# Expert weights through three pairs of buffers to the end, token rows in a ring of four, gate and up halves as 16 KB rows

## The reference, cut to what matters

```
for e in range(N_EXPERTS):                    # 32 experts, 520 tokens, D_MODEL 1024, D_EXPERT 256
    gu = xt @ w_gate_up[e]                    # 1024 x 512, f32: 2 MiB
    h = silu(gu[:, :D_EXPERT]) * gu[:, D_EXPERT:]
    y = y + gate[:, e:e + 1] * (h @ w_down[e])    # 256 x 1024, f32: 1 MiB
return layernorm(ALPHA * x1 + y)
```

## Time and profile before

| | us |
|---|---|
| median of 3 runs | 604.76 |
| the three runs | 601.89, 604.76, 605.17 |
| the profiled execution, its time | 602.56 |
| its span, first to last instruction | 600.9 |

### The profile page before, as it was taken

The page is one execution under the profiler, slowest core; times in us unless marked ns, Lnnn a source line. Parts: engine busy times, 40 slices in busy tenths (PEclk is TensorE's granted clock), DMA queues, the critical chain, the costliest instruction groups (busy, mean ns, idle before and its releaser), DMA issues.

```text
span 600.9 us, 8960 instructions
## 1 busy us (share of the span) xinstructions
PE 518.8 (86%) x3296; PEld 281.0 (47%) x3296; DVE 373.2 (62%) x722; ACT 191.4 (32%) x356; POOL 134.0 (22%) x156
## 2 busy tenths in 40 slices
PE   5999999999979879899999898888887777767761
PEld 4887788874355443445556743333332222222220
DVE  1642059898933576652258666677886477666686
ACT  0100374214243644121142122444444244432340
POOL 1001054500025760000000201233323222221231
PEclk9999999999979999999999899999999899999997
DMA  9940008570606932001978599999999999999951
GB/s 302 405 155 6 1 1 331 213 269 1 279 5 230 395 116 87 2 1 59 417 290 342 180 420 406 409 396 419 415 415 411 419 418 419 415 415 418 401 193 43
DMA packets 34010, 157.95 MB, mean 263 GB/s; under 512 B 12680, under 2 KB 12680, under 8 KB 20016
## 3 DMA queue, kind: packets, MB, share of 16 engines
q1 hardware_dynamic: 20592, 127.46, 52.9%
q0 software_dynamic: 10752, 29.59, 13.0%
q10 hardware_dynamic: 2624, 0.34, 0.4%
HBM read 160.12 MB, written 21.23 MB: 302 GB/s over the span
## 4 chain that ended last, share of the span: by engine, by line
PE 56%; DMA 26%; DVE 8%; ACT 7%; issue 3%; SPq 0%; POOL 0%; DVEq 0%; POOLq 0%; ACTq 0%
DMA arena_o<-in_w_gu 19%; PE ps L489 17%; PE ps L748 8%; PE ps L962 8%; PE ps L985 4%; PE ps L651 3%; PE ps L589 2%; PE ps L635 2%; DVE arena_s L1477 2%; PE ps L672 2%; DMA first_rows<-arena_s,known 1%; DMA x_rows<-arena_s 1%; PE ps L555 1%; DMA known<-slot_table 1%; DMA slot_table<-arena_s 1%
## 5 line engine op out<-in xcount | busy, mean ns | idle before, releaser
L962 PE MATMUL ps<-arena_w,arena_s 128*64 128x512 f32 x368 | 109.2, 605 | 24.1 <-DMA arena_w<-in_w_gu 12.3
L489 PE MATMUL ps<-arena_w 128*128 128x260 f32 x416 | 94.5, 388 | 6.7 <-DMA arena_w<-in_w_in 6.2
L489 PEld LDWEIGHTS ps<-arena_w 128*128 128x128 f32 x416 | 79.7, 193 | 21.0 <-DMA arena_w<-in_w_in 6.2
L962 PEld LDWEIGHTS ps<-arena_w,arena_s 128*64 128x64 f32 x368 | 33.2, 139 | 96.9 <-issue 66.4
L985 PE MATMUL ps<-arena_w,cs 128*64 128x512 f32 x184 | 56.1, 615 | 20.8 <-ACT cs L1260 20.8
L748 PE MATMUL ps<-arena_o,arena_s 128*128 128x512 f32 x128 | 58.3, 601 | 1.6 <-DVE arena_s L1601 1.6
L962 PE MATMUL ps<-arena_o,arena_s 128*64 128x512 f32 x112 | 50.2, 595 | 0.0
L1477 DVE STREAM_TRANSPOSE arena_s<-arena_w 128x1024 f32<-128x1024 f32 x36 | 41.8, 1214 | 8.3 <-PE ps L589 8.2
L2150 POOL DMA_INDIRECT first_rows<-arena_s,known x15 | 18.0, 1202 | 113.9 <-ACT arena_s L1267 105.1
L1910 DVE TENSOR_TENSOR arena_s<-arena_s,ps 128x256 f32<-128x256 f32 x16 | 6.7, 421 | 56.5 <-ACT arena_s L1256 56.5
L985 PEld LDWEIGHTS ps<-arena_w,cs 128*64 128x64 f32 x184 | 16.0, 141 | 51.0 <-issue 30.3
(11 more groups left out here) (349 smaller groups left out, 897.3 us busy)
## 6 DMA issues: line engine op xcount, KB each, us to landing
arena_w<-in_w_gu SPq DMA_DIRECT2D x46, 1024.0 KB, 19.9
arena_w<-in_w_dn SPq DMA_DIRECT2D x23, 1024.0 KB, 19.9
arena_o<-in_w_gu SPq DMA_DIRECT2D x14, 1024.0 KB, 23.2
arena_o<-in_w_dn SPq DMA_DIRECT2D x7, 1024.0 KB, 23.8
arena_w<-in_w_in SPq DMA_DIRECT2D x13, 512.0 KB, 14.1
arena_o<-in_w_out SPq DMA_DIRECT2D x1, 4096.0 KB, 13.5
arena_s<-in_w_gu SPq DMA_DIRECT2D x4, 1024.0 KB, 8.1
arena_w<-in_xT SPq DMA_DIRECT2D x4, 520.0 KB, 6.7
```

The costliest lines, as they stand in the source:

```text
L489: last = mm(ps[rows, b + n, 0:HALF], lhs(k), rhs(k)[:, n * HALF:(n + 1) * HALF], start=(k == 0), stop=(k == ks - 1))
L962: last = mm(ps[64 * e:64 * e + 64, 2 + q, :], xgT[:, k, CAP * e:CAP * (e + 1)], gu_w[2 * slots + e][:, k, :], start=(k == 0), stop=(k == K ...
```

## The change

- **Weights.** Pairs use the three pairs of buffers to the end, in the order 0, 1, 2, 0, 1, 0, 1, 2 from pair 3 on. A slot no longer holds an expert: one slot of a pair holds the first half of gate and up for both experts, the other the second half. In DRAM the two experts' halves lie side by side, so that a half of a pair is one transfer of 2 MiB with 16 KB for each partition. Down weights stay as they were.
- **Start.** Each of the first transfers into slots 2, 5, 3 and 4 is a half of a pair. That of slot 4 is issued right behind the last store of the norm's rows, ahead of the waits for the stores and for the first gather; slot 4's down weights stay behind them.
- **Rows.** The ring has four places. In step n GpSimd does: wait for the landing of output n-2 and gather rows n+2; scatter own half n; wait for the landing of output n-2 and scatter output n-1; gather other half n+1, which waits for the landing of own half n.
- **VectorE and ScalarE.** `finish(n-1)` and `root(n-1)` in step n in place of n-2. In the last pair the other half is added before the wait for the down products, and the products are added from PSUM behind it.
- **PE.** Five small matmuls behind the last gate and up products.
- **GpSimd.** The bound of the row numbers is kept in a register.

```
-S_XG = [5120, 6144, 0, D, S_RT] + [S_SLOT + D * n for n in range(3)]
-S_YO = [S_SLOT + 3 * D, 2 * D, S_SLOT + 4 * D]
+BUFFER = (0, 1, 2, 0, 1, 0, 1, 2)
+GU_SLOT = [[0, 1], [2, 3], [5, 4]]
+S_XG = [5120, 6144, 0, D]
+S_YO = [S_RT, 2 * D]
...
+def pair_buffer(n):
+    return n if n < HEAD else BUFFER[(n - HEAD) % BODY]
+
+def before_in(n):
+    d = 1
+    while BUFFER[(n - HEAD - d) % BODY] != pair_buffer(n):
+        d += 1
+    return d
...
         def ring(n):
-            return n % BODY
+            return n % 4
...
-            def gate_up(j, e, half):
-                cols = slice(half * KD * DE, (half + 1) * KD * DE)
-                sp.dma_start(gu_flat[j][:, cols], w_gu[e].rearrange("o p n -> p (o n)")[:, cols]).then_inc(gu_landed[half][j // 2], 16)
+            def gate_up(q, half, pr):
+                sp.dma_start(gu_flat[GU_SLOT[q][half]], w_gu[half, pr].rearrange("o p n -> p (o n)")).then_inc(gu_landed[half][q], 16)
...
             store_x1(4)
+            gate_up(2, 1, slice(2, 3))
             landed(sp, x1_stored, TT)
             landed(sp, gathered[0])
-            for half in range(2):
-                gate_up(4, slice(4, 5), half)
             down(4, slice(4, 5))
...
-            def refill(q, e, used):
-
+            def refill(it, n):
+                q, used = pair_buffer(n), nth(it, n, add=1 - before_in(n))
+                p = n if it is None or isinstance(it, tuple) else (it * BODY + n) % NPAIR
                 for half, done in enumerate((gu_half, gu_ps)):
                     sp.wait_ge(done, used)
-                    for n in range(2):
-                        gate_up(2 * q + n, slice(e + n, e + n + 1) if isinstance(e, int) else bass.ds(e + n, 1), half)
+                    gate_up(q, half, slice(p, p + 1) if isinstance(p, int) else bass.ds(p, 1))
...
-            refill(0, 6, 1)
-            refill(1, 8, 2)
+            refill(None, HEAD)
+            refill(None, HEAD + 1)
...
-            with sp.Fori(0, n_rounds * (NE // 4) - 3) as it:
-                refill(0, (it * 4 + 10) % NE, it * 2 + 4)
-                refill(1, (it * 4 + 12) % NE, it * 2 + 5)
-            refill(0, NE - 2, past + (NPAIR - 2))
+            with sp.Fori(0, n_rounds * 2 - 1) as it:
+                for n in range(HEAD + 2, HEAD + 2 + BODY):
+                    refill(it, n)
+            for n in range(HEAD + 2 + BODY, NPAIR):
+                refill((past,), n)
...
                 if not last_pair:
                     turn_tokens(it, n + 1)
+                else:
+                    for _ in range(5):
+                        mm(ps[:, 7, 0:P], ident[:, :], ident[:, :], start=True, stop=True)
...
-                if n >= 2:
-                    finish(it, n - 2)
+                if n >= 1:
+                    finish(it, n - 1)
                 own_part(it, n)
...
-            finish((past,), NPAIR - 3)
+            finish((past,), NPAIR - 2)
             hidden((past,), NPAIR - 1)
-            finish((past,), NPAIR - 2)
-            own_part((past,), NPAIR - 1, True)
-            finish((past,), NPAIR - 1)
+            finish((past,), NPAIR - 1, True)
...
             def pair_step(it, n):
-                scatter_own(it, n)
-                if n >= 3:
-                    outs, = number(nth(it, n - 2, 1, 16))
-                    fixed()
-                    pool.wait_ge(out_landed, outs)
-                if n >= 2:
-                    scatter_out(it, n - 2)
-                if n >= 1:
-                    gather_other(it, n)
-                if n == 1:
-                    pool.wait_ge(dn_ps, HEAD)
-                if n < HEAD:
-                    gather_rows(n + 4, first_at[:, n + 4:n + 5])
-                elif not isinstance(it, tuple) or n + 4 < NPAIR:
-                    there, = number(nth(it, n, QUAD, 16, 16))
+                m = n + 2
+                if n == 2:
+                    pool.wait_ge(out_landed, 16)
+                    gather_rows(m, first_at[:, m:m + 1])
+                elif n > 2 and (not isinstance(it, tuple) or m < NPAIR):
+                    there, gone = number(nth(it, m, QUAD, 16), nth(it, n, 1, 16, -16))
                     fixed()
                     pool.wait_ge(rows_at_landed, there)
-                    gather_rows(n + 4, rows_at.bitcast(I32)[:, (n + 4) // QUAD % 2, n % QUAD:n % QUAD + 1])
+                    pool.wait_ge(out_landed, gone)
+                    gather_rows(m, rows_at.bitcast(I32)[:, m // QUAD % 2, m % QUAD:m % QUAD + 1])
+                scatter_own(it, n)
+                if n >= 1:
+                    scatter_out(it, n - 1)
+                gather_other(it, n + 1)
...
-        "w_gu": i["w_gate_up"][pairs].reshape(NE, KD, P, 2 * DE).transpose(0, 2, 1, 3).reshape(NE, P, -1),
+        "w_gu": i["w_gate_up"][pairs].reshape(NE // 2, 2, 2, KD // 2, P, 2 * DE).transpose(2, 0, 4, 1, 3, 5).reshape(2, NE // 2, P, -1),
```

More of the change, by code:

```diff
@@ L417, in _ @@
             for half in range(2):
[L418 to L419 removed]
+                gate_up(0, half, slice(0, 1))
             for j in (0, 1):
                 down(j, slice(j, j + 1))
[L422 to L423 removed]
+            gate_up(1, 0, slice(1, 2))
             down(2, slice(2, 3))
@@ L427, in _ @@
             sp.wait_ge(dec_mixed, 1)
-            for half in range(2):
-                gate_up(5, slice(5, 6), half)
+            gate_up(2, 0, slice(2, 3))
             down(5, slice(5, 6))
@@ L432, in _ @@
             sp.wait_ge(o_done, 16)
-            for half in range(2):
-                gate_up(3, slice(3, 4), half)
+            gate_up(1, 1, slice(1, 2))
             down(3, slice(3, 4))
             store_x1(4)
+            gate_up(2, 1, slice(2, 3))
             landed(sp, x1_stored, TT)
             landed(sp, gathered[0])
-            for half in range(2):
-                gate_up(4, slice(4, 5), half)
             down(4, slice(4, 5))
@@ L2215, in _ @@
                 pair_step((past,), n)
-            n = NPAIR - 1
-            gather_other((past,), n)
-            for k in range(3):
-                scatter_out((past,), n - 2 + k)
-            fixed()
-            landed(pool, out_landed, n_rounds * NPAIR)
+            scatter_out((past,), NPAIR - 2)
+            ready, before, stored = number(nth((past,), NPAIR - 1, add=1), nth((past,), NPAIR - 1, 1, 16), n_rounds * (16 * NPAIR))
+            scatter_out((past,), NPAIR - 1, ready, before)
+            pool.wait_ge(out_landed, stored)
 def _lay_out(i):
```

86 lines of the change are left out of this document (46 added, 40 removed).

## The result

The changed kernel takes 655.65 us (median of 4 runs, 652.1 to 658.37), the kernel before beside it 604.96 (601.89 to 605.49): a ratio of 1.0846, interval [1.0775, 1.0917]. The direction and the place of the loss were as forecast; the size was not: 633 was the number, 600 to 651 the range. The profiled execution took 652.1 us, with a span of 650.5; the mean granted clock is 0.922, where it was 0.979.

What follows compares the result with a forecast made beforehand. Before the change, PE set the pace until about 455 us, then the weights; afterwards a row loop would. Pair 3's end at 418.7 + 11 x 17.2 + 13.4 + 10.1 tail + 1.7 gave 633 us, range 600 to 651.

Steps and rivals of the forecast that it cites:

- down products of pair 3 end: Start of the row loop: rows 4 land late, so these products end at 418.7 us instead of 398.9.
- eleven pairs, to the end of pair 14's: Steady part: 11 pairs at 17.2 us each, paced by the row loop through GpSimd.
- the last pair: Pair 15, with no rows to wait for: 13.4 us.
- tail, and what lies around the span: After the last down products: 10.1 us instead of 12.2, plus 1.7 us around the span.
- the term of a pair, 17.2 us: Half of a two-pair loop through output landing, row gather and PE, mixed over row sizes: 17.6, lowered to 17.2 us.
- the 6.7: PE's time from the transposes of new rows to the end of the down products: 6.7 us, from the earlier trace.
- the 0.8 a loop that was given back by hand: Allowance for a weight queue empty part of the time: 17.6 us a pair lowered to 17.2.
- the smaller of two prices: Small transfers beside 16 KB rows: the price giving 17.6 us a pair, taken over the one giving 19.1.
- Turns cost more: Rival, chance 0.17: small transfers pay more beside 16 KB rows, 19.1 us a pair less 0.5; 649 to 652 us.
- the main case: Likeliest case, chance 0.45: small transfers take turns of one weight row, the row loop sets the pace; 622 to 643 us.
- Row size costs nothing: Rival, chance 0.22: 16 KB rows cost small transfers nothing, only the late start remains; 600 to 614 us.
- Faster: Rival, chance 0.14: the row loop stays hidden and the weight queue decides; 592 us.

Runs made afterwards that it cites:

- d_warm28: Changed kernel with 28 small matmuls on PE ahead of the wait for rows of every second pair: 652.7 us, ratio 1.0839.
- g_tail: Kernel before with only the change's last pair (other half added before the down products, five small matmuls): 602.81 us, ratio 0.9995.
- a_8kb: Changed kernel with each half of a pair's gate and up weights sent as two transfers of 8 KB rows: 620.4 us, ratio 1.0307.

## Why the prediction was right in direction and wrong in size

The number is 22.7 us short. By its own steps, in the profiled execution:

| step | predicted | measured | error |
|---|---|---|---|
| down products of pair 3 end | 418.7 | 421.4 | +2.7 |
| eleven pairs, to the end of pair 14's | 189.2 | 201.5 | +12.3 |
| the last pair | 13.4 | 17.4 | +4.0 |
| tail, and what lies around the span | 11.8 | 11.8 | 0 |
| median over the profiled run | 0 | 3.5 | +3.5 |

**The start came out right, in part by luck.** Output 0, scatter 1 and the gather ahead of the rows came in the order forecast, and rows 4 landed at 412.2 (forecast 412). But they were issued at 400.67, not 405.4, and took 11.50 us, not 6.6, in a queue that was still full (0.99 from 400 to 410): two errors of near 5 us that cancel. What was late is what PE did with the rows: 9.2 us from landing to the end of the down products, where the sum had 6.7.

**The step that failed is the term of a pair, 17.2 us**, and it is the same 6.7 in it. From the output at 426.58 to that at 578.86 the chain goes four times round a loop of two pairs, 38.1 us each. Outputs landed in 12.5 us on average (12.90, 11.05, 12.02, 14.16), rows in 10.1 (5.83, 11.64, 9.95, 12.96), with 0.8 between them; from the landing of rows to the end of the down products are 9.6 us, and from there to the next output 5.0. The forecast loop was 35.2: 23.3 for landings and what lies between (measured 23.4), 5.2 (5.0) and 6.7 (9.6). So the landings in sum were right and the 6.7, read in the earlier trace rows from a PE at full clock that had not waited, was not the time of a PE that had. The 2.9 us are PE's own: on this chain the transposes take 1.9 us in the mean, the down products 5.8, where the chain of the kernel before has 1.04 and 3.65, and behind the warm matmuls of d_warm28 both are back at 1.04 and 3.65. The rest is the 0.8 a loop that was given back by hand. The prediction named this reading as one of the two on which it stands.

Two agreements in this are luck. By its own terms the forecast's 23.3 us were about 9.9 for the output and 12.7 for the rows behind it; measured are 12.5 and 10.1. And the error of a pair is larger than the table has it: ten pairs took 18.8 us each, and pair 14 took 13.6, since PE had the rows of pair 15 in time, where the forecast gave it 17.2 as well.

That the parts of this sum are the measured ones is shown. That the kernel would be 2.9 us a loop faster at full clock is not: d_warm28 restored the clock at five places, its pace is 0.2 us shorter, and its waits stand at other pairs. Whether full clock everywhere would give the rest wasn't tried.

**The last pair** took 17.4 us instead of 13.4. PE waits 3.3 us for VectorE (L994 behind L1927, the hidden half of pair 15), which stands in a row behind the output of pair 14, and the down products take 4.80 us behind this wait instead of 3.65. This follow-up of a late loop was not in the sum. Of the sum's 3.5 us for the tail, the 2.1 behind the last down products came (10.2 us against 10.1), though in the kernel before, as g_tail shows, they are not to be had; the 1.4 that the five small matmuls were to give did not, since PE waits behind them and the clock falls again (0.84 in the mean from 630 to 641).

**Row size.** The forecast had 2.8 us a pair between 8 and 16 KB rows (14.8 and 17.6); measured in the profiles are 1.9 (16.4 and 18.3), on a base that was too low by 1.6. The profile of a_8kb lies 9.3 us above the two executions that count, so that the true difference may be nearer to the forecast. The Trainium skill (DMA: Bandwidth & Descriptors, Queues, rings and completion order) has an engine drain a packet of typically 9 to 17 descriptors before it switches. The trace does not agree: from 550.5 to 562 us the two queues change after nearly every packet, as said above, one row a turn. The growth of the time with the size of the weight row would be there by either rule.

**Small slips.** 888 packets on 16 engines are 55.5 each, not 54; nothing rests on it. The store whose 7.8 us decided for the smaller of two prices was issued at 111.68, when the queue was still empty (share 0.00 from 111.6 to 112.6), so it says less than it was taken to say. The last fit that the prediction takes from the Trainium skill is stated there for transfers issued by GpSimd, and the weights are SyncE's; the sum does not use it.

**Third buffer and slot 4.** Nothing, as forecast, at 16 KB; the sign at other sizes was not asked for. That pair 8 behind pair 6 makes a hole was right; that it costs may be so at 4 KB (1.0041 and 0.9996, intervals that touch), and is not so at 8 and 16. The 5 us of slot 4 don't count, as the sum had it.

**The rivals.** "Turns cost more" (649 to 652) came nearest in time, but not by its mechanism: the landings of a loop took 23.4 us with what lies between, as the main case had, and not about 3 more. "Row size costs nothing" fell with a_8kb. "Faster" fell with the 55 us of waits for rows. The measured 655.65 lies above the range, as the loop had no term for what a wait does to the work behind it.

## What to carry to other kernels

Before a bulk stream is given larger rows, look for small transfers beside it that stand in a loop one behind another: here each of their turns waited for one row of the stream, and the same 16 KB rows that cost 1.1% in a kernel that fetches four pairs ahead cost 5.4 points in one where an output must land before the next gather may go. Look less at the distance of a ring than at what the issuing queue must wait for ahead of the fetch: with 8 KB rows two pairs ahead cost nothing in the old order (with 16 KB rows 1.5 points), and one place later in the queue, behind the scatter, 27%. And when you forecast work that will follow a wait, read its time from rows that follow a wait.

## What the runs showed of the hardware

The queue of GpSimd and that of SyncE took turns packet by packet (300 changes against 17 from 550.5 to 562 us), and a slot that moves no bytes took its turn like any other. More buffers for the stream can cost: a third one cost 6 to 12 us at 8 KB rows and gave 4 to 7 at 4 KB; at each size it filled the queue while the first scatter and output were on their way. Small matmuls in a wait brought PE back to full clock (transposes 1.04 us, down products 3.65) where the wait left behind them was short or none, and gave no time that the runs can show.

Smaller rows cost the stream little: 408 GB/s with 4 KB rows against 417 with 8 KB ones in a full queue, 2.2% for rows of half the size. With these rows and the buffers in regular order the new structure just reaches the kernel before (0.9996 [0.997, 1.0022]); no version tried beats it.
